# A two-layer hybrid trunk on one core: the attention layer rewritten token-major, four heads at a time, woven into its projections

## The chip, the cores and the metric
The kernel runs on one NeuronCore of a Trainium2 chip. The metric is the device time of one execution in microseconds (us); several runs are made and the median is compared. TensorE (PE) multiplies matrices into PSUM (eight banks of 512 float32 per partition), VectorE (DVE) and ScalarE (ACT) work on SBUF and PSUM, and SyncE (SP) issues the weight loads. Each engine runs its own list of instructions in order and waits on semaphores.

## The reference
256 tokens of width 1024 pass two layers, each a token mixer and a channel mixer, both after an RMS norm and with a residual add. Layer 0 is a gated linear recurrence and a dense SwiGLU; layer 1 is the attention that is changed here, and a top-2-of-8 expert SwiGLU. Then comes a last norm. The attention:

```python
qkv = h @ w_qkv + b_qkv                                   # 1024 -> 16*64 q, 4*64 k, 4*64 v
q, k = apply_partial_rope(q, cos, sin), apply_partial_rope(k, cos, sin)   # first 16 of 64 dims
scores = einsum('bnqkgd,bnjkd->bnkgqj', qb, kc) * 64 ** -0.5              # blocks of 128, own and previous
scores = where(allowed, scores, NEG_INF)                  # causal, window 128
probs = softmax(concatenate([scores, sink], -1), -1)[..., :-1]            # a learned sink per head
o = einsum('bnkgqj,bnjkd->bnqkgd', probs, vc)
return o @ w_o + b_o
```

All is float32. Four query heads share a key and value head.

## The kernel before, in words
The residual `h` lies feature-major: 8 chunks of 128 features by 256 tokens. All weights stream through a ring of 14 slots of 1 MB (a "piece" is a 1024x256 part of a weight matrix). The first part of the program uses seven of them; slots 7 to 10 serve it as scratch, and 11 to 13 hold split activations. The order of the work is written out by hand, one list per engine, with counting semaphores.

Two kinds of matmul are used. The recurrence, the attention and the router use plain float32 operands (`tile`, L1047: 8 matmuls of 128x256 for a 128x256 result; each float32 matmul shows as two instructions in the trace). The dense feed-forward part and the experts split weights and activations into a high and a low fp32r part: ACT casts a piece to `w_hi` (L469, L547), DVE subtracts to get `w_lo` (L747, L929), and TensorE makes three passes, hi*hi, lo*hi and hi*lo (`PASSES`; L1123, L1140, L1331, L1353). Three buffers (`PARTS`) hold split pieces, and a piece's split can begin once the piece three before it is used up (`parts_used`).

The stages in order: load of x and constants, rotary angles on DVE (L662 to L684) and the norm (to 29 us); the recurrence (to 136 us); 42 feed-forward pieces (to 374.5 us); norm and attention (to 537 us); norm, router and expert tables (to 568 us); eight experts of 42 pieces each; the last norm and the output. A norm is: ACT squares a chunk (L422), TensorE sums over partitions with a matrix of ones (L1038), ACT takes the root (L426), DVE the reciprocal (L708) and eight scaled chunks `hn` (L710).

The attention before: the K projection waits for `hn` and runs in `tile`; V is projected token-major with its bias by a matmul (L1174, L1178). K is copied to both halves of the partitions and rotated by constant matrices (L1182, L1185, then DVE L795 to L797). Then eight rounds, one for each pair of heads. A round projects the next pair's q (L1047), scores two heads (L1209, L1212; the two heads lie on partitions 0 to 63 and 64 to 127), adds the mask and takes row maxima on DVE (L814 to L818), exponentials on ACT (L512 to L514), normalises on DVE (L824 to L827), transposes the probabilities on TensorE (L1219), copies them on ACT (L518), rotates q (L1201), and weighs the values (L1228 to L1230). After the last round come 8 output tiles (L1047) with the residual add (L841) and the squares of the next norm between them.

The queue of the weight loads: expert pieces 0 to 6 wait for the attention's pieces to be used up, one by one, and pieces 7 to 13 for the router's first matmul, since their slots hold the attention's scratch.

## Time and profile before
| | us |
|---|---|
| median of 3 runs | 1601.21 (1601.06, 1601.21, 1609.16) |
| the profiled execution | 1610.67 |
| its span | 1608.9 |
| PE busy / DVE busy / ACT busy | 1518.0 / 1159.3 / 901.1 |
| mean granted TensorE clock | 0.969 |

The span is that of the profiled execution; 1.8 us lie around it. The median of the runs is 9.5 us under it. The page gives busy shares over the whole span; the stretch of the change is a tenth of it and has to be read on its own.

### The profile page before, as it was taken

Reading aid. Unit: us, or ns where it says so; the run is one execution under the profiler, and the core shown is the slowest. Engines: PE = TensorE matmul, PEld = TensorE weight load, DVE = VectorE, ACT = ScalarE, POOL = GpSimd, SP = SyncE. Lnnn points to the kernel's source line nnn. Section 1 sums busy time; section 2 is a strip of 40 time slices with the busy share of each in tenths; the row PEclk is TensorE's granted clock in tenths of the full one; section 3 lists DMA queues with packets and bytes.
Section 4 is the critical chain, followed back from the end, with each engine's and each line's share of the span. In section 5 each row is a group of like instructions: output and inputs, shape, how many; then the busy total and the mean of one; then the engine's idle time right before and its main releaser. Section 6 shows DMA issues by size and latency. Waiting matters only on the chain.

```text
span 1608.9 us, 25224 instructions
## 1 busy us (share of the span) xinstructions
PE 1518.0 (94%) x10533; PEld 1364.4 (85%) x10533; DVE 1159.3 (72%) x1225; ACT 901.1 (56%) x935; POOL 0.2 (0%) x4
## 2 busy tenths in 40 slices
PE   5989999998778799999999999999999999999995
PEld 4879999996556788989989898998898998898883
DVE  5564555552443488888888979979888988888883
ACT  2533444431233177676676766767767766766762
POOL 0000000000000000000000000000000000000000
PEclk9999999999879799999999999999999999999997
DMA  6436555551111589999989989999999999999910
GB/s 235 157 105 229 179 189 189 184 184 53 53 53 53 221 340 352 342 342 363 367 315 365 373 311 364 373 337 352 356 341 345 364 335 353 358 342 349 356 67 28
DMA packets 62058, 425.28 MB, mean 264 GB/s; under 512 B 7805, under 2 KB 10106, under 8 KB 10746
## 3 DMA queue, kind: packets, MB, share of 16 engines
q1 hardware_dynamic: 60240, 422.60, 70.9%
q8 instruction: 86, 1.41, 0.3%
q10 hardware_dynamic: 1706, 1.06, 0.2%
q14 instruction: 26, 0.21, 0.0%
HBM read 422.59 MB, written 1.05 MB: 263 GB/s over the span
## 4 chain that ended last, share of the span: by engine, by line
PE 90%; DVE 4%; ACT 3%; issue 2%; DMA 1%; ACTq 0%; DVEq 0%
PE ps L1331 37%; PE ps L1353 19%; PE ps L1123 10%; PE ps L1047 9%; PE ps L1140 5%; PE ps L1301 2%; PE ps L1319 2%; PE ps L1338 1%; PE ps L1038 1%; DVE w_lo L929 1%; ACT w_hi L547 1%; DVE ring L814 1%; PE ps L1178 0%; DVE hn L710 0%; PE ps L1267 0%
## 5 line engine op out<-in xcount | busy, mean ns | idle before, releaser
L929 DVE TENSOR_TENSOR w_lo<-ring,w_hi 128x2048 fp32r<-128x2048 f32 x336 | 766.4, 2290 | 126.7 <-ACT w_hi L547 121.0
L547 ACT CAST w_hi<-ring 128x2048 fp32r<-128x2048 f32 x336 | 639.5, 1909 | 264.6 <-PE ps L1331 213.5
L1331 PE MATMUL ps<-w_hi,xg_hi 128*96 128x256 f32 x1792 | 246.9, 280 | 2.5 <-ACT w_hi L547 2.5
L1331 PE MATMUL ps<-w_lo,xg_hi 128*96 128x256 f32 x1792 | 242.2, 277 | 1.6 <-DVE w_lo L929 1.6
L1331 PE MATMUL ps<-w_hi,xg_lo 128*96 128x256 f32 x1792 | 241.8, 277 | 0.0
L1331 PEld LDWEIGHTS ps<-w_hi,xg_hi 128*96 128x96 f32 x1792 | 221.6, 162 | 15.9 <-DVE xg_lo L935 2.6
L1331 PEld LDWEIGHTS ps<-w_lo,xg_hi 128*96 128x96 f32 x1792 | 215.1, 161 | 3.2 <-DVE w_lo L929 3.2
L1331 PEld LDWEIGHTS ps<-w_hi,xg_lo 128*96 128x96 f32 x1792 | 216.1, 162 | 0.0
L747 DVE TENSOR_TENSOR w_lo<-ring,w_hi 128x2048 fp32r<-128x2048 f32 x42 | 96.2, 2293 | 80.7 <-ACT w_hi L469 80.7
L469 ACT CAST w_hi<-ring 128x2048 fp32r<-128x2048 f32 x42 | 79.9, 1904 | 105.0 <-PE ps L1123 98.8
L1353 PE MATMUL ps<-w_hi,ht_hi 128*96 128x512 f32 x448 | 128.0, 407 | 0.0
L1353 PE MATMUL ps<-w_lo,ht_hi 128*96 128x512 f32 x448 | 122.4, 394 | 0.0
L1353 PE MATMUL ps<-w_hi,ht_lo 128*96 128x512 f32 x448 | 122.4, 395 | 0.0
L1047 PE MATMUL ps<-hn,ring 128*128 128x256 f32 x416 | 105.8, 419 | 13.5 <-issue 9.0
L1047 PEld LDWEIGHTS ps<-hn,ring 128*128 128x128 f32 x416 | 87.8, 213 | 30.8 <-issue 16.7
L1353 PEld LDWEIGHTS ps<-w_lo,ht_hi 128*96 128x96 f32 x448 | 71.9, 161 | 32.5 <-DVE w_lo L929 0.6
L1353 PEld LDWEIGHTS ps<-w_hi,ht_lo 128*96 128x96 f32 x448 | 72.2, 161 | 31.4
L1353 PEld LDWEIGHTS ps<-w_hi,ht_hi 128*96 128x96 f32 x448 | 63.7, 162 | 16.2
L422 ACT ACTIVATE xg_mem<-h 128x256 f32<-128x256 f32 x40 | 16.3, 415 | 76.1 <-DVE h L841 27.6
L1123 PE MATMUL ps<-u_hi,w_hi 128*128 128x256 f32 x448 | 57.5, 281 | 0.0
L1123 PE MATMUL ps<-u_lo,w_hi 128*128 128x256 f32 x448 | 57.3, 281 | 0.0
L1123 PE MATMUL ps<-u_hi,w_lo 128*128 128x256 f32 x448 | 57.3, 281 | 0.0
(235 smaller groups left out, 1373.8 us busy)
## 6 DMA issues: line engine op xcount, KB each, us to landing
ring<-in_moe_w_gate SPq DMA_DIRECT2D x112, 1024.0 KB, 5.8
ring<-in_moe_w_up SPq DMA_DIRECT2D x112, 1024.0 KB, 5.9
ring<-in_moe_w_down SPq DMA_DIRECT2D x112, 1024.0 KB, 5.8
ring<-in_ffn_w_gate SPq DMA_DIRECT2D x14, 1024.0 KB, 4.9
ring<-in_ffn_w_up SPq DMA_DIRECT2D x14, 1024.0 KB, 4.9
ring<-in_ffn_w_down SPq DMA_DIRECT2D x14, 1024.0 KB, 4.8
ring<-in_lru_w_in SPq DMA_DIRECT2D x8, 1024.0 KB, 7.9
ring<-in_attn_w_qkv SPq DMA_DIRECT2D x6, 1024.0 KB, 4.9
```

The source lines that it names most:

```text
L422: nc.scalar.activation(sq[:, c % 2], h[:, c], ACT.Square).then_inc(sq_ready, 1)
L469: nc.scalar.copy(w_hi[:, j % PARTS], ring[:, slot_of[FIRST_FFN + j]]).then_inc(hi_done, 1)
L547: nc.scalar.copy(w_hi[:, (SPLITS + n) % PARTS], ring[:, s]).then_inc(hi_done, 1)
L747: V.tensor_tensor(w_lo[:, j % PARTS], ring[:, slot_of[FIRST_FFN + j]], w_hi[:, j % PARTS].bitcast(F32), ALU.subtract).then_inc(lo_done, 1)
L929: V.tensor_tensor(w_lo[:, part], ring[:, ORDER_MOE[n % SLOTS]], w_hi[:, part].bitcast(F32), ALU.subtract).then_inc(lo_done, 1)
L1047: mm = nc.tensor.matmul(ps[:, bank, c0:c0 + T], w[:, k, col:col + P], rhs[:, k], start=(k == 0), stop=(k == KC - 1))
L1123: mm = nc.tensor.matmul(ps[:, 2 * (c % 2) + f, m * T:(m + 1) * T], w[b][:, k, f * P:(f + 1) * P], us[a][:, k], start=(k == 0 and (a, b) == ...
L1140: mm = nc.tensor.matmul(ps[:, 4 + d // 2, (d % 2) * T:(d % 2 + 1) * T], w[b][:, f, d * P:(d + 1) * P], fs[a][:, c % 2, f], start=False, st ...
L1301: mm = nc.tensor.matmul(ps[:, SCATTER_BANK[m], (d % 2) * T:(d % 2 + 1) * T], y_tok[:, d * P:(d + 1) * P], gt, start=True, stop=True)
L1319: mm = nc.tensor.matmul(ps[:, 4 + g, m * CAP:(m + 1) * CAP], hn_tok[:, b, c * P:(c + 1) * P], sel[:, b], start=(b == 0), stop=(b == TT - 1))
L1331: mm = nc.tensor.matmul(ps[0:CAP, c % 2, m * CHF:(m + 1) * CHF], xs[a][:, k], w[b][:, k], start=(k == 0 and (a, b) == (0, 0)), stop=(k == ...
L1353: mm = nc.tensor.matmul(ps[0:CAP, 2 + g, :], hs[a][:, c % 2, f], w[b][:, f, g * 512:(g + 1) * 512], start=(c == 0 and f == 0 and (a, b) == ...
```

## The change
- The norm before the attention is no longer applied ahead of the projections. ACT makes, for each chunk as it is finished, its square and `u_hi` (the chunk times the norm's weight, cast), and DVE `u_lo`; the projections run on these, and 1/rms is applied per token when their results are evicted. The sum of squares is 16 float32 matmuls with a single moving column (`mean_squares`), inside the K projection.
- All ten pieces of `w_qkv` and `w_o` go through the hi/lo split and three passes, as the feed-forward pieces do. The last feed-forward piece goes output chunk by output chunk.
- Q, K and V are projected token-major, so the bias is an operand of the eviction (loaded once, broadcast, 0.8 MB) and the rotation touches 16 of each 64 columns; the angle tables shrink from 256 columns to 16. The rotation matrices and the duplicating matrices go.
- K is written twice side by side, transposed, and stored with one half of the partitions zero, so a score matmul takes all 128 partitions. The mask is added by a bf16 matmul with the identity. Four heads of a group are scored into three PSUM banks; row maxima and exponentials read PSUM.
- Probabilities are transposed unnormalised, the values come out token-major, and one DVE instruction normalises a group. The heads are transposed back, and split into `heads_hi` and `heads_lo`.
- Four rounds instead of eight, with the Q projections, and parts of the output projections, in between, in the order listed in the diff.
- The expert loads 0 to 6 wait for the splits of attention pieces 3 to 9, and 7 to 13 for the use of the last one.

The core of the diff (`project`, `evict`, `rope`, `row_max`, `empty_probs`, `normalise`, `split_heads` and `turn_*` are as described):

```diff
-SPLITS = FFN_LOADS
+SPLITS = FFN_LOADS + ATT_LOADS
...
-                if FIRST_FFN <= last < FIRST_ATT:
+                if last >= FIRST_FFN:
                     sp.wait_ge(lo_done, last - FIRST_FFN + 1)
-                elif last >= FIRST_ATT:
-                    sp.wait_ge(used, last - FFN_LOADS + 1)
...
-                    if first and n < SLOTS:
-                        sp.wait_ge(used, LRU_LOADS + min(ATT_LOADS, ATT_LOADS - DENSE + n + 1))
+                    if first and n < DENSE:
+                        sp.wait_ge(lo_done, SPLITS - DENSE + n + 1)
+                    elif first and n < SLOTS:
+                        sp.wait_ge(parts_used, SPLITS)
...
+            split_att(0)
+            split_att(1)
+            for c in range(KC):
+                act.wait_ge(h_ready, 2 * KC + c + 1)
+                nc.scalar.activation(sq_all[:, c], h[:, c], ACT.Square).then_inc(att_sq, 1)
+                nc.scalar.activation(u_hi[:, c], h[:, c], ACT.Copy, scale=param("mix1", c)).then_inc(att_u_hi, 1)
+            split_att(2)
+            act.wait_ge(att_sum, 1)
+            nc.scalar.activation(rms2, ps[:, 7, 0:TT], ACT.Sqrt, bias=eps_col, scale=1.0 / D).then_inc(att_rms, 1)
+            split_att(3)
+            split_att(4)
+            split_att(5)
...
+            def soften(g):
+
+                st = stat[:, 64 * (g % 2):64 * (g % 2) + 64]
+                act.wait_ge(negmax, 2 * g + 1)
+                for n in range(GROUP):
+                    nc.scalar.activation(probs[:, 0, n * P:(n + 1) * P], ps[:, 2, n * P:(n + 1) * P], ACT.Exp, scale=HD ** -0.5,
+                                         bias=st[:, 8 + n:9 + n], accum_out=st[:, 16 + n:17 + n]).then_inc(exp_done, 1)
...
+            empty_q(0)
+            soften(0)
+            split_att(6)
+            empty_q(1)
+            empty_last_probs(0)
+            soften(1)
+            split_att(7)
+            empty_q(2)
+            empty_last_probs(1)
+            soften(2)
+            cast_heads(0)
+            empty_q(3)
+            empty_last_probs(2)
+            soften(3)
+            cast_heads(1)
+            cast_heads(2)
+            split_att(8)
+            empty_last_probs(3)
+            cast_heads(3)
+            split_att(9)
...
+            split_att(0)
+            split_att(1)
...
+                dve.wait_ge(att_u_hi, c + 1)
+                V.scalar_tensor_tensor(out=u_lo[:, c], in0=h[:, c], scalar=param("mix1", c), in1=u_hi[:, c].bitcast(F32),
+                                       op0=ALU.mult, op1=ALU.subtract).then_inc(att_u, 1)
+            split_att(2)
+            dve.wait_ge(att_rms, 1)
+            link(V.reciprocal(rstd2, rms2))
+            for m in range(2):
...
+            def evict(a, out, col):
+                dve.wait_ge(parts_used, FFN_LOADS + a + 1)
+                for b in range(TT):
+                    V.scalar_tensor_tensor(out=out[:, b], in0=ps[:, a % 2, b * T:(b + 1) * T].rearrange("p (h d) -> p h d", d=HD),
+                                           scalar=rstd2[:, b:b + 1], in1=bias_row[:, col:col + T].rearrange("p (h d) -> p h d", d=HD),
+                                           op0=ALU.mult, op1=ALU.add).then_inc(qkv_evac, 1)
...
+            evict(K_PIECE, k_tok, D)
+            rope(K_PIECE, k_tok)
...
+            split_att(3)
+            evict(V_PIECE, v_tok, D + NKV * HD)
+            split_att(4)
+            for g in range(2):
+                evict(Q_PIECE + g, q_tok[:, g], T * g)
+                rope(Q_PIECE + g, q_tok[:, g])
+                if g == 0:
+                    empty_k(0)
+                    empty_k(1)
+                    split_att(5)
+            row_max(0)
+            evict(Q_PIECE + 2, q_tok[:, 0], 2 * T)
+            rope(Q_PIECE + 2, q_tok[:, 0])
+            split_att(6)
+            empty_probs(0)
+            row_max(1)
+            normalise(0)
+            evict(Q_PIECE + 3, q_tok[:, 1], 3 * T)
+            rope(Q_PIECE + 3, q_tok[:, 1])
+            split_att(7)
+            empty_probs(1)
+            row_max(2)
+            normalise(1)
+            split_heads(0)
+            empty_probs(2)
+            row_max(3)
+            normalise(2)
+            split_heads(1)
+            split_att(8)
+            split_heads(2)
+            empty_probs(3)
+            normalise(3)
+            split_heads(3)
...
-                dve.wait_ge(wo_proj, c + 1)
-                V.scalar_tensor_tensor(out=h[:, c], in0=ps[:, c % 4, 0:T], scalar=param("b_o", c), in1=h[:, c],
...
+                dve.wait_ge(parts_used, FFN_LOADS + O_PIECE + c // 2 + 1)
...
+                last = c == NCH - 1
+                if last:
+                    pe.wait_ge(lo_done, j + 1)
+                    order = [(a, b, d) for d in range(KC) for a, b in PASSES]
...
+            def mean_squares():
+                pe.wait_ge(att_sq, KC)
+                for b in range(TT):
+                    for c in range(KC):
+                        mm = nc.tensor.matmul(ps[:, 7, b:b + 1], sq_all[:, c, b * P:(b + 1) * P], const("ones")[:, 0:1],
+                                              start=(c == 0), stop=(c == KC - 1))
+                mm.then_inc(att_sum, 1)
+
+            def project(a):
+                w = att_parts(a)
+                us = (u_hi, u_lo)
+                if a >= 2:
+                    pe.wait_ge(qkv_evac, 2 * (a - 2) + 2)
+                open_bank(a % 2)
+                for m, n in PASSES:
+                    if n:
+                        pe.wait_ge(lo_done, FFN_LOADS + a + 1)
+                    for k in range(KC):
+                        if a == 0 and n == 0:
+                            pe.wait_ge(att_u if m else att_u_hi, k + 1)
+                        for b in range(TT):
+                            mm = nc.tensor.matmul(ps[:, a % 2, b * T:(b + 1) * T], us[m][:, k, b * P:(b + 1) * P], w[n][:, k],
+                                                  start=False, stop=(k == KC - 1 and n == 1), skip_group_check=True)
+                    if a == 0 and m:
...
+                    if m:
+                        mask, each, heads_in = mask_bf[:, P:3 * P], 2, (2 * m - 2, 2 * m - 1)
+                    else:
...
+                    nc.tensor.matmul(ps[:, 2 + m, :], ident_bf, mask.unsqueeze(1).to_broadcast([P, each, width]),
+                                     start=True, stop=False, skip_group_check=True)
+                    for at, n in enumerate(heads_in):
+                        q_cols = slice(P, 2 * P) if m else slice(0, P)
+                        mm = nc.tensor.matmul(ps[:, 2 + m, at * width:(at + 1) * width], q_fm[:, g % 2, n // 2, q_cols],
+                                              kd[:, g, n % 2, 0:width], start=False, stop=True, skip_group_check=True)
...
+            def project_out(t, ks):
+                a = O_PIECE + t
+                w = att_parts(a)
+                hs = (heads_hi, heads_lo)
+                if 0 in ks:
+                    if t == 0:
+                        pe.wait_ge(qkv_evac, 2 * (Q_PIECE + 3) + 2)
+                    else:
+                        pe.wait_ge(exp_done, 9 * NKV)
+                    open_bank(WO_BANK[t])
+                pe.wait_ge(*emptied("h", max(ks) // 2))
+                for m, n in PASSES:
+                    if n:
+                        pe.wait_ge(lo_done, FFN_LOADS + a + 1)
+                    for f in range(2):
+                        for k in ks:
+                            mm = nc.tensor.matmul(ps[:, WO_BANK[t], f * T:(f + 1) * T], w[n][:, k, f * P:(f + 1) * P], hs[m][:, k],
+                                                  start=False, stop=(k == KC - 1 and n == 1), skip_group_check=True)
+                if KC - 1 in ks:
+                    mm.then_inc(parts_used, 1)
+
...
+            project(K_PIECE)
+            project(V_PIECE)
+            project(Q_PIECE)
+            turn_k(0)
+            turn_k(1)
+            project(Q_PIECE + 1)
+            turn_q(0)
+            score(0)
+            project(Q_PIECE + 2)
+            turn_q(1)
+            turn_probs(0)
+            score(1)
+            weigh_values(0)
+            project(Q_PIECE + 3)
+            turn_q(2)
+            turn_probs(1)
+            score(2)
+            weigh_values(1)
+            turn_heads(0)
+            turn_q(3)
+            project_out(0, (0, 1))
+            turn_probs(2)
+            score(3)
+            weigh_values(2)
+            turn_heads(1)
+            project_out(0, (2, 3))
+            turn_heads(2)
+            turn_probs(3)
+            project_out(0, (4, 5))
+            weigh_values(3)
+            project_out(1, range(6))
+            turn_heads(3)
+            project_out(2, range(6))
+            for t in range(3):
+                project_out(t, (6, 7))
+            for c in range(4):
+                sum_square(2, c, 7)
+            project_out(3, range(KC))
+            for c in range(4, KC):
+                sum_square(2, c, 7)
```

## Rows read from the trace of the kernel before
**Rows 1.** The page: granted clock in 40 slices; a costly group (busy, mean ns).
```profile
PEclk9999999999879799999999999999999999999997
...
L469 ACT CAST w_hi<-ring 128x2048 fp32r<-128x2048 f32 x42 | 79.9, 1904 | 105.0 <-PE ps L1123 98.8
```

**Rows 2.** Busy time by stretch: length, PE, PEld, DVE, ACT, POOL (instructions), clock, DMA share, GB/s.
```profile
200.00:220.00 20.00, 20.00 (x172) 20.00 (x171) 11.15 (x10) 8.53 (x8) 0.00 (x0) 1.00 0.57 204
...
374.50:544.90 170.40, 129.75 (x599) 100.94 (x598) 66.04 (x195) 45.30 (x137) 0.00 (x0) 0.87 0.17 56
...
440.90:452.60 11.70, 9.22 (x42) 6.85 (x42) 5.72 (x19) 3.92 (x14) 0.00 (x0) 0.71 0.17 50
...
544.90:551.70 6.80, 6.80 (x33) 6.80 (x33) 0.00 (x0) 0.00 (x0) 0.00 (x0) 0.50 0.75 283
...
600.00:650.00 50.00, 50.00 (x369) 45.31 (x368) 44.20 (x35) 33.60 (x27) 0.00 (x0) 1.00 0.96 355
```

**Rows 3.** Timeline, end of the dense feed-forward part: start, us, engine, line, operation.
```profile
359.78 2.29 DVE L747 TENSOR_TENSOR w_lo<-ring,w_hi 128x2048 fp32r<-128x2048 f32 x1 [3.36 <-ACT w_hi L469]
...
372.66 2.05 PE L1140 MATMUL ps<-f_hi,w_lo 128*128 128x256 f32 x16
373.33 2.74 DVE L788 TENSOR_TENSOR h<-ps,h 128x256 f32<-128x256 f32 x8 [6.80 <-PE ps L1140]
...
385.65 9.31 PE L1047 MATMUL ps<-hn,ring 128*128 128x256 f32 x32 [6.28 <-issue]
```

**Rows 4.** Timeline where the feed-forward part gets its split activations today.
```profile
118.94 0.42 DVE L754 TENSOR_TENSOR h<-ps,h 128x256 f32<-128x256 f32 x1 [2.55 <-PE ps L1047]
...
119.40 0.42 ACT L422 ACTIVATE xg_mem<-h 128x256 f32<-128x256 f32 x1 [3.47 <-DVE h L754]
...
119.79 0.48 DVE L758 SCALAR_TENSOR_TENSOR u_lo<-h,par,u_hi 128x256 fp32r<-128x256 f32 x1
```

**Rows 5.** Timeline in the attention, rounds of two heads.
```profile
419.71 0.50 PE L1209 MATMUL ps<-ring 64*128 64x128 f32 x4
...
420.04 0.61 PE L1212 MATMUL ps<-ring 64*128 64x256 f32 x4
...
421.47 0.41 DVE L817 TENSOR_REDUCE ring<-ring 128x1 f32<-128x256 f32 x1
...
422.17 0.40 ACT L512 ACTIVATE ring<-ring 128x128 f32<-128x128 f32 x1 [0.57 <-DVE ring L818]
...
422.57 0.49 ACT L513 ACTIVATE ring<-ring 128x256 f32<-128x256 f32 x1
...
424.16 5.30 PE L1047 MATMUL ps<-hn,ring 128*128 128x256 f32 x16
...
430.25 0.65 PEld L1219 LDWEIGHTS ps<-cst,ring 128*128 128x128 f32 x6 [0.33 <-issue]
...
485.69 3.72 PE L1047 MATMUL ps<-hn,ring 128*128 128x256 f32 x16
```

**Rows 6.** Timeline, the last norm and the router.
```profile
537.38 0.42 ACT L422 ACTIVATE xg_mem<-h 128x256 f32<-128x256 f32 x1 [3.47 <-DVE h L841]
...
544.88 6.97 PE L1267 MATMUL ps<-wr,hn 128*128 128x8 f32 x32 [6.33 <-DVE hn L710]
...
551.70 3.65 PE L1274 MATMUL ps<-cst,hn 128*128 128x128 f32 x16
...
552.65 0.22 DVE L858 TENSOR_TENSOR xg_mem<-small 128x64 f32<-128x64 f32 x1
...
552.87 0.57 ACT L539 COPY work<-ps 128x512 f32<-128x512 f32 x1
```

**Rows 7.** Timeline, start of the program: the rotary angles and the first evictions of x.
```profile
10.69 0.29 DVE L662 CAST ring<-ring 128x256 f32<-128x256 int32 x1
...
17.59 2.73 DVE L687 COPY h<-ps 128x256 f32<-128x256 f32 x8
```

**Rows 8.** Waits of the SyncE queue in the expert stage: total us, times, longest.
```profile
SPq L373 <- DVE w_lo L929: 489.4, 205, 5.7
```

505 lines of the change are left out of this document (251 added, 254 removed), and 3 rows, old and new, of the table TURNS.

## The prediction, made before the changed kernel was run
> **What bounds the kernel now.** I read the page's slices first [rows 1]: each is 40 us, and the granted clock dips in slices 11, 12 and 14 (402 to 563 us, the attention and the router) and at the very end; elsewhere it is near full. Busy time by stretch comes next [rows 2]. In the feed-forward part TensorE is busy 20.00 of 20 us, with 172 instructions (0.116 us each); in the experts 50.00 of 50 us. There the weight queue waits for the DVE splits that free slots, 489.4 us in 205 waits [rows 8], and not the other way round, so the loads keep ahead. The experts neither gain nor lose unless their first pieces come late. The stretch of the attention, from 374.5 to 544.9 us, is different: 170.4 us with TensorE busy 129.8, a clock of 0.87, DVE busy 66 and ACT 45. No engine is full; it is a chain of handoffs, and the low clock comes with the waits: in one round (11.7 us) TensorE is busy 9.2 us at 0.71 [rows 2]. So the change has to be priced as a chain from the end of the feed-forward part (374.5) to the router's first matmul (544.88), and all times below are on the clock of this trace.
>
> **Durations used.** A three-pass piece is 48 matmuls of 0.116 us and an opening matmul (0.2), 5.8 us; two plain tiles take 2 x 3.72 = 7.4 [rows 2, 5]. At the low clock (0.50, 1.2 GHz) a weight load of 128 columns takes 6.97/32 = 0.218 us, at the full one 0.65/6 = 0.108 [rows 5, 6], a factor of two, which I use for all matmuls. So at full clock a transpose costs 0.11, a float32 matmul with a narrow moving operand two loads, 0.22, one of 256 columns 3.72/8 = 0.465, one of 128 about 0.23. A split is 1.9 on ACT and 2.29 on DVE [rows 1, 3]. ACT empties 128x512 in 0.57 [rows 6]; for DVE I take 0.6. An exponential costs 0.40 (128 columns) and 0.49 (256), a maximum 0.41 for 256 columns, so 0.65 for 512 [rows 5]. A small DVE operation is 0.22 [rows 6]. A bf16 matmul of 512 columns has no row of its own; I take two loads, 0.21, and between 0.1 and 0.465 it moves a round by under 1 us.
>
> **Step 1, into the K projection.** Before: first residual add at 373.33, K at 385.65 [rows 3]. Now DVE must add a chunk, wait for ACT's square and cast, and subtract, and its next add is queued behind that subtraction. From the feed-forward entry [rows 4]: add to ACT start 0.46, then 0.42 twice, handoff 0.05, subtraction to next add 0.4: 1.76 us a chunk. The reordering of the last piece releases chunks from 370.5 on, but DVE first does the splits of attention pieces 0 and 1, and the second may start only when the last but one piece is used (369): ACT 1.9 and DVE 2.3 end at 373.3, so nothing is earlier. The two DMA issues that ACT makes for sinks and bias move ahead of the feed-forward pieces, where ACT waits for TensorE before its next cast; they cost nothing, nor does their 0.8 MB. Eight chunks end at 387.3. The first pass follows chunk by chunk and hides in it. The new wait on `lo_done` ahead of the last piece costs nothing: that split ends at 359.78 + 2.29 = 362.07, before the piece starts [rows 3].
>
> **Step 2, the rest of K.** TensorE has mostly waited for 13 us, so it starts low. 16 matmuls x 0.232 = 3.7; the mean squares 32 instructions, 7.0 low, 3.5 full; the last pass 3.7 low, 1.9 full. Rows for both exist: the K tiles of before rise within their 9.31 us [rows 3], while the router's 32 narrow instructions stay at 0.50 for all 6.8 us, and 16 transposes after them take 3.65 [rows 2, 6]. `mean_squares` is narrow like the router, so I take low: 14.4 us, to 401.7; bounds 9.1 and 14.4.
>
> **Step 3, to the first scores.** V and Q0 11.6, four blocks of K transposed 8 x 0.11 = 0.9, Q1 5.8, four transposes, an ACT copy and two handoffs 1.2, scores of a group 3 x 0.21 + 4 x 0.23 + 4 x 0.465 = 3.4: 22.9, to 424.6. DVE's evictions (2 x 0.48), rotation (six small operations, 1.5), K copies and splits run beside the projections, about 17 us of work in 23. The root's table load falls beside them too; where it doesn't, it costs 1.3.
>
> **Step 4, two full rounds.** A round is a projection (5.8), 16 transposes with handoffs (2.0), scores (3.4), values (12 float32 matmuls, 24 x 0.108 = 2.6). Row maxima (2.2) and exponentials (4 x 0.40 + 4 x 0.49 + 0.28 = 3.8) hide under the projection: 3.1 us of them come after the scores, against 5.8. But DVE, after the projection, evicts and rotates (2.5), splits (2.3) and empties two banks (1.2), 6.0 against TensorE's 5.4 to the values: 0.6 of wait. 14.4 each, to 453.4; heads and q transposes 0.9.
>
> **Step 5, rounds three and four.** No Q projection is left to hide the softmax, only 12 matmuls (1.4) at a time. DVE is free at 450.8: maxima 2.2, exponentials' second half 2.2, cast 0.6, subtraction 0.65, handoffs 0.2: 456.7. Matmuls 1.4, transposes 1.3, scores 3.4 (462.8), values 2.6. Tail of the maxima 0.9, then 2.2 + 0.6 + 0.65 + 0.2: 467.4, TensorE waits 1.2. 1.4 and 0.4 of matmuls and transposes: 469.2. Then a queue effect: the subtraction of heads 2 stands behind the split of piece 8 on DVE, and the third bank of transposes of round four waits for it: 0.6 + 1.9 + 2.3 + 0.65 + 0.1 gives 474.7, 5 us of wait. 1.8 and the values 2.6: 479.1. Two output pieces over six chunks 8.8 and transposes 0.4: 488.3; piece 0 is complete at 489.7.
>
> **Step 6, the tail.** The split of piece 9 needs piece 0 used up: 1.9 + 2.3 + 0.1, 494.0. Four adds stand behind it on DVE (1.6), the fourth square and sum 0.9, last piece 5.8: 502.3; two more adds, and the last square starts at 503.3. From there to the router it is 544.88 - 537.38 = 7.5 as before [rows 6]: 510.8.
>
> **Clock in the rounds.** This has TensorE at full clock from 402 on. Before, a wait of 2 to 3 us cost the next tile 5.30 - 3.72 = 1.6 us [rows 5]. I count three waits over 2 us (steps 5 and 6) and smaller ones: 6 us; bounds 0 and, at the 0.8 of the old rounds on 60 us of work, 15. Router at 516.8, 28.1 us earlier.
>
> **Start.** The angle chain on DVE, 10.69 to 17.59 [rows 7], is about 17 linked operations of 256 columns; at 0.2 each they take 3.6, and the copies of mask and identity add 0.7: 2.6 us earlier, all on the path, as the evictions of x stand behind it; bounds 0 and 4.
>
> **Expert loads.** Pieces 7 to 13 are released at 502, ahead of the router rather than with it, and take some 20 us of a DMA queue at 355 GB/s [rows 2] against 29 us to the first expert matmul: nothing.
>
> **Sum.** 28.1 + 2.6 = 30.7 us: 1610.7 gives 1580 for an execution like the profiled one. The median of the runs is 9.5 us under it and two of three agree within 0.2 us, so I take 1601.2 - 30.7 = 1570.
>
> **A rule against the change.** A pair of heads scored on two partition halves takes 419.71 to 420.65, 0.94 us [rows 5]; on the full array the same matmuls are 1.4 by the durations above, 3.6 us more over eight pairs, which is in the sum. The Trainium skill (TensorEngine Tiling (Array Packing), Theoretical Speedup) says that a contraction of 64 or less gains up to a factor of two from row tiling, which this change gives up; by it the loss is an estimated 8 x 0.94 = 7.5 us instead, and the time 1574. The case's rows show a factor of 1.5.
>
> **Rivals.** (a) *The clock comes back early*: full after step 2's first pass, no loss in the rounds, and the start gives 4: 5.3 + 6 + 1.4 = 13 less, 1557. For: TensorE's gaps are shorter than before. Against: the router's row. (b) *The elementwise chains set the rounds*: linked DVE operations and PSUM reads cost 3 us more in each of four rounds and the clock stays at the old 0.8, 12 + 9 more, 1591. For: DVE has 6.0 against 5.4 already in step 4. (c) *Slower*: TensorE stays at 1.2 GHz for the rounds, because transposes and narrow matmuls don't lift it. For: the router and the transposes after it [rows 2, 6]. Against: 288 wide matmuls of the q, k, v pieces lie between them, and the old rounds, with fewer, had 0.71 to 0.9. Price: about 84 us of TensorE work on the path doubles, less the 6 counted: 1648. It decides once 37 of the 84 us run low. The Trainium skill (TensorE: Matmul & The Clock Gate, Part 4: PE-mode transpose) says transposes don't count as busy for the clock; here 88 of them are under 10 us of the work. (d) *The gain is eaten* by several waits: within 8 us of before.
>
> **Chances.** Forecast 0.48, (a) 0.20, (b) 0.22, (c) 0.06, (d) 0.04. About 0.5% (8 us) is what a measurement can tell. Faster 0.90, same 0.04, slower 0.06. The range 1552 to 1596 takes in (a), (b) and the bounds of steps 2, the clock and the start.
>
> **What would show it.** Step 1: adds 1.7 to 1.8 us apart, K's first pass ending near 387. Step 2: the mean squares at 7 or 3.5 us. Step 4: rounds of 14 to 15 us. Step 5: a TensorE wait near 5 us for the subtraction behind the split of piece 8. The router near 517, or 514 with the start counted; the expert stage as long as before. Wrong would be rounds over 18 us, a clock under 0.7 in them, or a first expert matmul that waits for a load.

## The result and the profile after

The kernel after took 1591.8 us in the median of 8 runs (1588.5 to 1597.0), the kernel before 1602.4 (1600.9 to 1609.2): a ratio of 0.993, with 0.991 to 0.995 as its interval. It is 10.5 us faster; 31 were forecast (1570), and the time is inside the range. The profiled execution of after took 1589.4, that of before 1610.7, 21.3 apart: seven of the eight executions of before lie at 1600.9 to 1602.6 and one at 1609.2, and the profiled one, which is not among the eight, was of that upper kind.

The page of after: the span, the granted clock in 40 slices, and the groups of the feed-forward cast and of the experts' gate and up matmuls (busy us, mean ns).

```profile
span 1587.5 us, 25538 instructions
...
PEclk8999999997998899999999999999999999999997
...
L1527 PE MATMUL ps<-w_hi,xg_hi 128*96 128x256 f32 x1792 | 252.1, 282 | 2.5 <-ACT w_hi L585 2.5
L1527 PE MATMUL ps<-w_lo,xg_hi 128*96 128x256 f32 x1792 | 248.2, 279 | 0.5
...
L484 ACT CAST w_hi<-ring 128x2048 fp32r<-128x2048 f32 x52 | 99.0, 1905 | 123.5 <-PE ps L1239 98.4
```

The same groups of the experts on the page of before, which the prediction did not look at:

```profile
L1331 PE MATMUL ps<-w_hi,xg_hi 128*96 128x256 f32 x1792 | 246.9, 280 | 2.5 <-ACT w_hi L547 2.5
L1331 PE MATMUL ps<-w_lo,xg_hi 128*96 128x256 f32 x1792 | 242.2, 277 | 1.6 <-DVE w_lo L929 1.6
```

Code, shape and count are the same, and 1792 matmuls are busy 252.1 us instead of 246.9. The cast of 2048 columns did not change (1905 ns against 1904 in [rows 1]).

Busy time by stretch of after, columns as in [rows 2]: feed-forward, attention, one round, router, experts.

```profile
200.00:220.00 20.00, 20.00 (x173) 20.00 (x172) 10.51 (x10) 8.99 (x8) 0.00 (x0) 1.00 0.62 208
369.10:508.20 139.10, 114.76 (x800) 103.90 (x799) 69.23 (x140) 50.38 (x116) 0.00 (x0) 0.89 0.25 89
430.60:444.60 14.00, 14.00 (x110) 13.12 (x110) 8.47 (x22) 6.33 (x21) 0.00 (x0) 1.00 0.23 74
508.20:515.10 6.90, 6.90 (x33) 6.90 (x34) 0.00 (x0) 0.00 (x0) 0.00 (x0) 0.50 1.01 425
600.00:650.00 50.00, 50.00 (x373) 45.75 (x372) 41.47 (x33) 33.11 (x27) 0.00 (x0) 1.00 0.93 340
```

The attention went from 170.4 us to 139.1, and TensorE waits 24 us in it instead of 41. A round of four heads takes 14.0 us with TensorE busy all the time at clock 1.00, where a round of two took 11.7 at 0.71 [rows 2]. In the last window after even has more instructions than before (373, 369 in [rows 2]), though its experts are slower: 50 us hold another part of an expert, with other shapes, in each kernel. A longer stretch, 900 to 1300 us, shows the loss. Before, then after:

```profile
900.00:1300.00 400.00, 399.30 (x2912) 359.12 (x2911) 344.75 (x256) 279.80 (x237) 0.00 (x0) 1.00 0.94 352
```

```profile
900.00:1300.00 400.00, 399.77 (x2869) 360.86 (x2868) 340.28 (x255) 276.08 (x234) 0.00 (x0) 1.00 0.92 342
```

TensorE is full and its clock 1.00 in both, yet 43 instructions fewer (1.5%) fit into 400 us. The 50 us windows are useless for this, and the busy share hides it altogether. From the first expert matmul to the end of the span before took 1608.9 - 568.0 = 1040.9 us and after 1587.5 - 531.7 = 1055.8. So the account of the profiled executions is 36.3 us gained up to the first expert matmul and 14.9 lost behind it.

The timeline of after (start, duration), to be held against [rows 3, 6]: the chunks, K's second pass, the mean squares, K's third pass and V's first, the queue effect, and the router.

```profile
367.73 0.42 DVE L835 TENSOR_TENSOR h<-ps,h 128x256 f32<-128x256 f32 x1
369.03 0.48 DVE L837 SCALAR_TENSOR_TENSOR u_lo<-h,par,u_hi 128x256 fp32r<-128x256 f32 x1 [0.88 <-ACT u_hi L515]
369.43 0.42 DVE L835 TENSOR_TENSOR h<-ps,h 128x256 f32<-128x256 f32 x1
...
381.54 3.62 PE L1309 MATMUL ps<-w_hi,u_lo 128*128 128x256 f32 x16
384.95 3.89 PE L1292 MATMUL ps<-cst,hn 128*128 128x1 f32 x32
388.71 3.59 PE L1309 MATMUL ps<-w_lo,u_hi 128*128 128x256 f32 x16
...
392.57 2.18 PE L1309 MATMUL ps<-w_hi,u_hi 128*128 128x256 f32 x16
...
463.14 2.29 DVE L788 TENSOR_TENSOR w_lo<-ring,w_hi 128x2048 fp32r<-128x2048 f32 x1 [4.70 <-ACT w_hi L484]
465.35 0.68 DVE L912 TENSOR_TENSOR u_lo<-ps,u_hi 128x512 fp32r<-128x512 f32 x1
...
466.18 1.08 PE L1367 MATMUL ps<-cst,ring 128*128 128x128 f32 x4 [4.62 <-DVE u_lo L912]
...
508.17 6.96 PE L1465 MATMUL ps<-wr,hn 128*128 128x8 f32 x32 [6.30 <-DVE hn L751]
```

The adds are 1.70 us apart, since each waits behind a subtraction that waits for ACT; the wait of 4.62 us stands where DVE splits piece 8 first; the router starts 36.7 us earlier than in [rows 6].

The experts' matmuls, in blocks of 8, timeline of before and then of after; the step from one start to the next is what a block costs.

```profile
958.69 1.08 PE L1331 MATMUL ps<-w_hi,xg_hi 128*96 128x256 f32 x8
959.61 1.07 PE L1331 MATMUL ps<-w_hi,xg_lo 128*96 128x256 f32 x8
960.51 1.07 PE L1331 MATMUL ps<-w_lo,xg_hi 128*96 128x256 f32 x8
961.42 1.09 PE L1331 MATMUL ps<-w_hi,xg_hi 128*96 128x256 f32 x8
```

```profile
957.64 1.10 PE L1527 MATMUL ps<-w_hi,xg_lo 128*96 128x256 f32 x8
958.58 1.10 PE L1527 MATMUL ps<-w_lo,xg_hi 128*96 128x256 f32 x8
959.52 1.10 PE L1527 MATMUL ps<-w_hi,xg_hi 128*96 128x256 f32 x8
960.47 1.10 PE L1527 MATMUL ps<-w_hi,xg_lo 128*96 128x256 f32 x8
```

0.91 us a block before (0.1135 a matmul), 0.945 after (0.118). There are 3 x 1792 = 5376 of these matmuls; 0.0045 us each would be 24 us. The stage loses less, 15 to 16, because before has slow blocks too: of the fourteen groups of six blocks in an expert, the first behind the scatter and two or three others run at 0.93 and the rest at 0.91; after has none at 0.91. What picks these groups is open. No wait of TensorE grew to account for the loss.

### The profile page after: what moved, and what is told of

Read it like the earlier page. It is cut to its first block, busy times and chain, and to the rows that moved or that the text cites. A ratio compares the mean times of both kernels' runs of the same rounds, so it can differ in the third digit from the quotient of the medians.

```text
span 1587.5 us, 25538 instructions
## 1 busy us (share of the span) xinstructions
PE 1516.6 (96%) x10735; PEld 1382.9 (87%) x10735; DVE 1164.2 (73%) x1173; ACT 909.1 (57%) x919; POOL 0.2 (0%) x4
## 3 DMA queue, kind: packets, MB, share of 16 engines
q8 instruction: 86, 1.41, 0.3%
## 4 chain that ended last, share of the span: by engine, by line
PE 90%; DVE 5%; ACT 4%; issue 1%; DMA 1%; ACTq 0%; DVEq 0%
PE ps L1527 38%; PE ps L1549 20%; PE ps L1239 10%; PE ps L1261 5%; PE ps L1163 4%; PE ps L1309 2%; PE ps L1497 2%; PE ps L1515 2%; PE ps L1414 1%; PE ps L1534 1%; DVE w_lo L1045 1%; ACT w_hi L585 1%; PE ps L1154 1%; DVE w_lo L788 1%; PE ps L1358 0%
## 5 line engine op out<-in xcount | busy, mean ns | idle before, releaser
L1045 DVE TENSOR_TENSOR w_lo<-ring,w_hi 128x2048 fp32r<-128x2048 f32 x336 | 766.7, 2290 | 141.5 <-ACT w_hi L585 137.3
L585 ACT CAST w_hi<-ring 128x2048 fp32r<-128x2048 f32 x336 | 638.8, 1907 | 279.5 <-PE ps L1527 228.9
L1527 PE MATMUL ps<-w_hi,xg_hi 128*96 128x256 f32 x1792 | 252.1, 282 | 2.5 <-ACT w_hi L585 2.5
L1527 PE MATMUL ps<-w_lo,xg_hi 128*96 128x256 f32 x1792 | 248.2, 279 | 0.5
L1527 PE MATMUL ps<-w_hi,xg_lo 128*96 128x256 f32 x1792 | 248.0, 279 | 0.0
L1527 PEld LDWEIGHTS ps<-w_lo,xg_hi 128*96 128x96 f32 x1792 | 220.8, 161 | 2.2 <-DVE w_lo L1045 2.2
L1527 PEld LDWEIGHTS ps<-w_hi,xg_lo 128*96 128x96 f32 x1792 | 221.7, 161 | 0.0
L788 DVE TENSOR_TENSOR w_lo<-ring,w_hi 128x2048 fp32r<-128x2048 f32 x52 | 119.1, 2292 | 96.8 <-ACT w_hi L484 96.7
L484 ACT CAST w_hi<-ring 128x2048 fp32r<-128x2048 f32 x52 | 99.0, 1905 | 123.5 <-PE ps L1239 98.4
L1549 PE MATMUL ps<-w_hi,ht_hi 128*96 128x512 f32 x448 | 127.9, 407 | 0.0
L1163 PE MATMUL ps<-hn,ring 128*128 128x256 f32 x256 | 58.5, 392 | 4.5 <-DVE hn L751 3.5
L1163 PEld LDWEIGHTS ps<-hn,ring 128*128 128x128 f32 x256 | 50.3, 197 | 12.5 <-issue 5.3
L1239 PEld LDWEIGHTS ps<-u_hi,w_hi 128*128 128x128 f32 x448 | 54.7, 188 | 0.1
```

Of the source, the lines that this page charges most:

```text
L484: nc.scalar.copy(w_hi[:, j % PARTS], ring[:, slot_of[FIRST_FFN + j]]).then_inc(hi_done, 1)
L585: nc.scalar.copy(w_hi[:, (SPLITS + n) % PARTS], ring[:, s]).then_inc(hi_done, 1)
L788: V.tensor_tensor(w_lo[:, j % PARTS], ring[:, slot_of[FIRST_FFN + j]], w_hi[:, j % PARTS].bitcast(F32), ALU.subtract).then_inc(lo_done, 1)
L1045: V.tensor_tensor(w_lo[:, part], ring[:, ORDER_MOE[n % SLOTS]], w_hi[:, part].bitcast(F32), ALU.subtract).then_inc(lo_done, 1)
L1163: mm = nc.tensor.matmul(ps[:, bank, c0:c0 + T], w[:, k, col:col + P], rhs[:, k], start=(k == 0), stop=(k == KC - 1))
L1239: mm = nc.tensor.matmul(ps[:, 2 * (c % 2) + f, m * T:(m + 1) * T], w[b][:, k, f * P:(f + 1) * P], us[a][:, k], start=(k == 0 and (a, b) == ...
```

## What could make the same instructions slower

The change inserts `mask_mem` (1024 bytes a partition) ahead of `xg_hi` and shrinks the constants `cst` by 2532 bytes. Buffers lie one behind the other in the order of their declaration, each start rounded up to 32 bytes. So `xg_hi` moved from byte 162432 to 163456 and `w_hi` from 179904 to 178400, and the distance between the two operands that a gate or up matmul reads went from 17472 to 14944 bytes. `xg_lo` and `w_lo` lie 3072 and 24576 bytes behind their partners in every kernel, so all three passes have the same distance modulo 256. My theory was the alignment of w; the rivals were another effect of the addresses, and the place of the instructions in TensorE's program or the phase in which the experts start.

### Three layouts (e1, e2, e3)

e1, in the kernel after:

```diff
         table = sb("table", [1, 2 + MAX_OVER], I32)
+        sb("pad", [P, 8])
```

> The kernel after, with 32 unused bytes per partition between `table` and `w_hi`, so that `w_hi` starts at byte 178432 (a multiple of 64) instead of 178400 and `w_lo` at 203008 instead of 202976; nothing else moves. In the trace of after the attention gave 31 us and the start 5.6, but the time only 10.5: the gate and up matmuls of the experts take 0.118 us each against 0.1135 before, though their code is unchanged. Theory 1 (the address of the split weights within 64 bytes; before has 179904, a multiple of 64): blocks of 8 gate/up matmuls back at 0.907 to 0.91 us, 5376 matmuls save 15 to 25 us, time 1567 to 1576. Theory 2 (another address effect: the distance from xg to w, or xg itself): blocks stay at 0.944, time 1588 to 1597. Theory 3 (place of the instructions in TensorE's program, or the phase in which the experts start): blocks stay at 0.944, time 1588 to 1597.

e2, in the kernel after, `mask_mem` moved:

```diff
-        mask_mem = sb("mask_mem", [P, 4 * P], BF16)
...
         cst = sb("cst", [P, NCONST])
+        mask_mem = sb("mask_mem", [P, 4 * P], BF16)
+        sb("pad", [P, 376])
```

> The kernel after, with every buffer that the experts use at its address of before: `mask_mem` is put behind `cst`, and 1504 unused bytes behind it, so that xg, ht, par, small, wr, table, w_hi (179904) and w_lo (204480) start where they did. Theory 1 (alignment of w) and theory 2 (any other address effect): gate/up blocks of 8 matmuls at 0.907 to 0.91 us as in the kernel before, time 1567 to 1576. Theory 3 (instruction stream or phase): blocks stay at 0.944, time 1588 to 1597.

e3, in the kernel before, the same line as in e1:

> The kernel before, with 32 unused bytes per partition between `table` and `w_hi`, so that w_hi and w_lo start 32 bytes behind a multiple of 64, as in the kernel after; nothing else moves. Theory 1 (alignment of w within 64 bytes): gate/up blocks go from 0.91 to 0.944 us, the time from 1601 to between 1616 and 1627. Theory 2 (another address effect) and theory 3 (instruction stream or phase): within 4 us of 1601.

Measured: e1 1589.5 us (4 runs), 2 us under after, where 15 to 25 were expected of it: alignment of w to 64 bytes is not it. e2 1568.4 (1561.9 to 1575.6, 4 runs; ratio to before 0.978, 0.973 to 0.983): within 2 us of the forecast, with the changed kernel's code and the old addresses. That it comes so close is partly luck, since the four runs are two near 1562 and two near 1575, and the median lies between them. e3 1622.8 against 1603.0 for before on the same chip, a ratio of 1.010 (1.007 to 1.014): 32 bytes make the old kernel 20 us slower. The stretch of 900 to 1300 us, e2 and then e3:

```profile
900.00:1300.00 400.00, 399.19 (x2918) 359.41 (x2917) 343.73 (x258) 279.73 (x236) 0.00 (x0) 1.00 0.93 350
```

```profile
900.00:1300.00 400.00, 399.76 (x2869) 360.88 (x2868) 339.55 (x251) 275.09 (x232) 0.00 (x0) 1.00 0.93 346
```

Each kernel shows the other's count within 6. That settles that addresses do it, in both directions, and rules out the instruction stream and the phase: e2 and after hold the same instructions, and e3 and before.

A part of e2's profiled execution is not the experts'. Its feed-forward stage took 230.9 us, against 238 to 241 in all other kernels, with blocks of 16 matmuls at 1.81 instead of 1.88 to 1.90; the window of 200 to 350 us of e2 holds

```profile
200.00:350.00 150.00, 150.00 (x1326) 150.00 (x1325) 88.33 (x85) 64.97 (x66) 0.00 (x0) 1.00 0.57 195
```

and that of after x1281. Other kernels in the same layout (e9 to e12 below) have 1.88 or 1.89, so this comes and goes from one execution to the next. These are the two prices of the experts once more (0.113 and 0.118 a matmul), at one and the same layout. The distance from `u_hi` to `w_hi`, which this stage reads, is 64, 96, 128 or 192 modulo 256 in the kernels of this document, and all but this execution of e2 have 1.88 to 1.90. So in the feed-forward stage the layouts tried do not decide the price; what does is open. That the shorter feed-forward stage makes the 11 us between the two faster and the two slower runs of e2 is likely by its size, but not shown.

### Which address (e5, e6, e7)

e5 and e6 start from e2, with the line below ahead of `xg_hi`; e5 takes its 32 bytes off the pad behind `mask_mem` again, e6 doesn't. e7 is e1 with 24 in place of 8.

```diff
+        sb("pad_xg", [P, 8])
         xg_hi, xg_lo = sb("xg_hi", [P, KC, CAP], F32R), sb("xg_lo", [P, KC, CAP], F32R)
```

> The kernel after in the layout of before, but with xg_hi to ht_lo (the stationary operands of the experts) 32 bytes further on and w_hi and w_lo where they were in before. Absolute alignment of w decides: gate/up blocks stay at 0.91 us, span 1560 to 1574. The distance from the stationary operand to w, or the alignment of the stationary operand, decides: 0.944 us, span 1576 to 1592.

> The same with everything from xg_hi to w_lo 32 bytes further on, so that all distances between them are those of before. Distance decides: gate/up blocks at 0.91 us, span 1560 to 1574. Absolute alignment of w decides: 0.944 us, span 1576 to 1592.

> The kernel after with 96 unused bytes ahead of w_hi: it starts at 178496, which is 64 past a multiple of 128 as in the kernel before (179904), while 178400, 178432 and 179936, all slow, are 96, 0 and 96 past one; xg stays where after has it. If w's place within 128 bytes decides (or its distance from xg within 128 bytes, which is then that of before too): gate/up blocks at 0.91 us and a median of 1565 to 1575. If the place of xg or of w in a larger unit decides: 0.944 us and 1588 to 1597.

The pads ahead of `xg_hi` move ht, `cst` and `mask_mem` with it. Moving xg alone costs the stage 13 us, moving w alone (e3) 16, and moving both costs nothing: it is the distance between the two operands. e7 met neither expectation cleanly, with blocks of 0.91 and 0.93, a stage 4 to 5 us longer than the best, and 1579.1 us. All layouts, with the stage from the first gate or up matmul of the experts to the start of their last block of 8 (profiled execution), and the instruction count of TensorE from 900 to 1300:

```
kernel           xg_hi    w_hi     distance  mod 256  stage us  count   time us (runs)
before           162432   179904   17472      64       996.5    2912    1602.4 (8)
e2 (after)       162432   179904   17472      64       995.8    2918    1568.4 (4)
e6 (after)       162464   179936   17472      64       997.3    2909    1581.8 (1)
e13 (after)      163456   178624   15168      64       996.8    2921    1574.5 (6)
e7 (after)       163456   178496   15040     192      1001.3    2908    1579.1 (4)
e5 (after)       162464   179904   17440      32      1009.0    2880    1588.6 (1)
e1 (after)       163456   178432   14976     128      1010.8    2877    1589.5 (4)
e3 (before)      162432   179936   17504      96      1012.2    2869    1622.8 (4)
after            163456   178400   14944      96      1012.4    2869    1591.8 (8)
```

From one contraction chunk to the next the moving operand steps by 1024 bytes and the stationary one by 384, so the distance grows by 640, which is 128 modulo 256. A layout at 64 thus alternates between 64 and 192, and so does one at 192, in the other phase: the two good ones. The others never meet 64 or 192. The stage repeats well: e9 to e12, in the layout of e2, took 996.5 to 996.9, and the kernels of the two scans below, in that of after, 1012.4 each. The times of the last column do not compare as well: e5, e6 and e7 ran where before took 1609.3 in the median, and single runs differ by their attention. That of e6 took 143.7 us to the router, against 136.5 in e2, because TensorE's clock stayed at 0.50 from K's third chunk to past K's end, 24 us without a break:

```profile
375.10:398.80 23.70, 19.12 (x80) 17.29 (x81) 9.48 (x21) 8.81 (x14) 0.00 (x0) 0.50 0.13 45
```

### The two reads with nothing else at work (e4, e8)

Behind the last expert, blocks of matmuls that differ only in where their operands start (e4: 24 matmuls a block; e8: 12, and more offsets). The core of e8:

```diff
+            for cols, src, pitch in ((128, wl, 256), (96, xf, 96)):
+                for so in range(0, 128, 8):
+                    for mo in range(0, 128, 8):
+                        for r in range(12):
+                            k = r % 6
+                            (even, odd)[n_scan % 2](ps[0:cols, 0, 0:256], src[:, so + k * pitch:so + k * pitch + cols],
+                                                    wf[:, mo + k * 256:mo + (k + 1) * 256])
```

> The kernel after with 64 blocks of 24 matmuls (256 moving columns from w_hi) added behind the last expert, where no other engine works: 32 with a stationary operand of 96 columns from xg_hi, 32 with one of 128 columns from w_lo; the first column of the moving operand goes through 8 offsets of 32 bytes, that of the stationary one through 4. They add about 64 x 24 x 0.116 = 178 us. If the effect of the addresses lies in TensorE's own two reads (weights and moving operand), blocks differ by offset, 2.72 us against 2.83 (0.1135 and 0.118 a matmul), in a pattern that repeats with the offset. If it comes from DVE, ACT or DMA writing the neighbouring parts at the same time, all blocks are alike here.

> As in the scan before, behind the last expert and with no other engine at work, but 512 blocks of 12 matmuls: the first column of the stationary and of the moving operand each go through 16 offsets of 32 bytes (0 to 480), first with a stationary operand of 128 columns from w_lo (202976; both pitches 1024 bytes), then with the experts' 96 columns from xg_hi (163456, pitch 384). In the first scan the fast blocks (2.73 us for 24, against 2.80 to 2.88) lay on a diagonal: at 128 columns where the moving offset was 192 bytes more than the stationary one, at 96 columns where it was 96 more. If the distance of the two reads modulo 512 decides: 128 columns fast (1.36 us for 12 against 1.41) in 16 blocks on one wrapped diagonal and nowhere else. If it is modulo 256, on two diagonals. If the absolute address counts beside the distance, the diagonal has gaps.

In e4 most blocks took 2.80 to 2.87 us and seven 2.72 or 2.73: four with 96 columns where the moving offset is 96 bytes more than the stationary one, two with 128 columns where it is 192 more, and the first block with 96 columns and the stationary offset 32.

Three blocks of e8, with 96 columns and the stationary offset 160, moving offsets 224, 256 and 288, and the next one:

```profile
2057.31 1.57 PE L1615 MATMUL ps<-w_hi,xg_hi 128*96 128x256 f32 x12
2058.71 1.53 PE L1612 MATMUL ps<-w_hi,xg_hi 128*96 128x256 f32 x12
2060.08 1.57 PE L1615 MATMUL ps<-w_hi,xg_hi 128*96 128x256 f32 x12
2061.49 1.56 PE L1612 MATMUL ps<-w_hi,xg_hi 128*96 128x256 f32 x12
```

1.40, 1.37 and 1.41 us from start to start. The block times in units of 0.01 us for 96 columns, stationary offset down, moving offset across, in steps of 32 bytes (first half of six of the 16 rows; the second half of each repeats it within 0.01, save for the 136 at the start of row 32, which is 142 there):

```
stationary 0     142 142 140 137 141 140 140 142
stationary 32    136 142 142 140 137 141 140 140
stationary 64    140 142 141 142 141 136 141 141
stationary 96    140 140 142 141 142 141 136 141
stationary 128   141 140 140 142 141 142 141 136
stationary 160   136 141 141 139 142 142 142 140
```

The fast blocks lie on a diagonal that wraps after 256 bytes: moving offset minus stationary offset is 96, a distance of 14944 + 96 = 15040 bytes, 192 modulo 256, as in all 32 places of the scan that have it. Two more blocks are as fast without it, the first of the rows 32 and 288; the moving offset has just jumped back from 480 to 0 there. With 128 columns all 9 fast blocks (1.37 or 1.38) are at 192 modulo 256 too, but the other 23 places with that remainder are at 1.40 to 1.42, among them one of the two where e4 had its fast ones. So the modulus I expected (512) was wrong, and the gaps say that the distance is not everything. What is shown: with DVE, ACT and the weight queue idle, the same matmul with 96 stationary columns costs 0.114 or 0.118 us by the distance of its two operands. The Trainium skill (SBUF — State Buffer, "SBUF: two separate sides") places contention at the port that DVE and GpSimd share and at the DMA side alone, and gives TensorE two read ports, one for the moving operand and one for the weight load, which it calls independent. By that the distance between the two should cost nothing; in the scan, with neither of the two places at work, it costs 2 to 4%. That it is these two reads meeting in the memory is my reading; the scan doesn't show the memory. Nor does it explain why the experts do best at 64 while the idle blocks do best at 192.

### A new distance with the old remainder (e13)

e1 with 56 in place of 8, all else that of after.

> The kernel after, unchanged but for 224 unused bytes ahead of w_hi, which make the distance from xg_hi to w_hi 15168 bytes: 64 more than a multiple of 256, as 17472 was before, though 2304 bytes shorter. So far the experts' gate/up stage (first to last gate/up matmul) took 996 to 997 us at 17472 bytes (64 modulo 256), 1001 at 15040 (192), 1009 at 17440 (32), 1011 at 14976 (128) and 1012 at 14944 and 17504 (96). Theory (the distance counts modulo 256): 996 to 998 us, blocks of 8 at 0.91, and a median of 1570 to 1576 (after less 16 us; nothing is gained in the attention, where another pair of operands is read). Rival (the exact distance, or the neighbours that share the old layout): over 1001 us, and 1579 or more.

Stage 996.8 us, as forecast, and 1574.5 us in 6 runs, ratio to before 0.980 (0.976 to 0.983): 224 unused bytes are worth 17 us to the kernel after. For this stage neither the exact distance nor the neighbours matter.

## Was the attention priced rightly (e9 to e12)

Four runs in the layout of e2, on the waits that the prediction's steps 1, 2 and 5 named. For them I give the time from the end of the feed-forward stage to the router's first matmul, 139.1 us in after and 136.5 in e2. These are single executions, and nine with the attention of after took between 136.5 and 143.7, so e2 is the shortest of its kind and 2 us are nothing. The spread comes from two places: K's last matmul stands 23 us behind the feed-forward stage in six of them and 26 in three (e6, e8, e13), whose clock stayed low as shown above, and the rest differs by two or three.

e9:

```diff
             split_heads(1)
-            split_att(8)
             split_heads(2)
             empty_probs(3)
+            split_att(8)
             normalise(3)
```

> The layout of before (the run e2, router's first matmul 139 us after the feed-forward part as in after), and on DVE the split of piece 8 moved behind the subtraction of heads 2 and the two bank copies of round four. Theory (step 5 of the prediction: the wait of 4.6 us for that subtraction is a queue effect of the 2.29 us split): the wait goes, the router comes 2.3 to 4.6 us earlier after the end of the feed-forward part. Rival (the output pieces set the end: piece 8's split, now later, is waited for): the same wait turns up ahead of the output piece 8 and the router stays within 1 us.

The wait fell from 4.6 us to 0.62, in e9's timeline (1568.6 us, one run):

```profile
461.08 0.69 DVE L913 TENSOR_TENSOR u_lo<-ps,u_hi 128x512 fp32r<-128x512 f32 x1 [2.86 <-ACT u_hi L549]
...
461.91 0.63 PE L1368 MATMUL ps<-cst,ring 128*128 128x128 f32 x4 [0.62 <-DVE u_lo L913]
```

and no new wait came ahead of piece 8: the queue effect is as told. From the end of the feed-forward stage the router came only 2.0 us sooner (134.5). Ahead of the edit e9 was already 2.6 us later than e2, in part by a first pass of V at the low clock, 2.83 us against 2.15; that is not the edit's doing. What the edit is worth shows from the eight transposes just ahead of the wait: from there to the router it is 41.1 us in e9 and 45.6 to 47.6 in the ten executions with the old order, 4 to 6 us less.

e10:

```diff
-                dve.wait_ge(att_u_hi, c + 1)
-                V.scalar_tensor_tensor(out=u_lo[:, c], in0=h[:, c], scalar=param("mix1", c), in1=u_hi[:, c].bitcast(F32),
-                                       op0=ALU.mult, op1=ALU.subtract).then_inc(att_u, 1)
+                for d in ([c - 1] if c else []) + ([c] if c == KC - 1 else []):
+                    dve.wait_ge(att_u_hi, d + 1)
+                    V.scalar_tensor_tensor(out=u_lo[:, d], in0=h[:, d], scalar=param("mix1", d), in1=u_hi[:, d].bitcast(F32),
+                                           op0=ALU.mult, op1=ALU.subtract).then_inc(att_u, 1)
```

> The layout of before, and DVE adds the residual of chunk c+1 before it subtracts for u_lo of chunk c. Theory (step 1 of the prediction: the next add queues behind a subtraction that waits for ACT, 1.70 us a chunk): chunks 1.0 to 1.2 us apart, K's second pass 4 to 5 us earlier, and the router 4 to 5 us earlier after the end of the feed-forward part, or more where TensorE's clock stays up. Rival (the splits of pieces 2 and 3 or the low clock after the gap set the time): chunks closer, but the router within 1.5 us.

```profile
368.87 0.42 DVE L836 TENSOR_TENSOR h<-ps,h 128x256 f32<-128x256 f32 x1
369.85 0.42 DVE L836 TENSOR_TENSOR h<-ps,h 128x256 f32<-128x256 f32 x1
370.18 0.48 DVE L839 SCALAR_TENSOR_TENSOR u_lo<-h,par,u_hi 128x256 fp32r<-128x256 f32 x1
370.57 0.42 DVE L836 TENSOR_TENSOR h<-ps,h 128x256 f32<-128x256 f32 x1
```

The adds now alternate between 0.72 and 0.98 us, 0.85 in the mean, closer than expected, and the router comes at 130.1, 6.4 us sooner than in e2 and outside the spread (1563.6 us, one run). K's last matmul stands 16.7 us behind the feed-forward stage, 6 less than the shortest without the edit. The 1.76 us a chunk of step 1 was a queue effect too, and the change left 6 us lying there.

e11 is e9 and e10 together. e12 adds the mean squares in the gaps, in a bank of their own (3) that is opened ahead of them:

```diff
-                pe.wait_ge(att_sq, KC)
+                pe.wait_ge(att_sq, c + 1)
                 for b in range(TT):
-                    for c in range(KC):
-                        mm = nc.tensor.matmul(ps[:, 7, b:b + 1], sq_all[:, c, b * P:(b + 1) * P], const("ones")[:, 0:1],
-                                              start=(c == 0), stop=(c == KC - 1))
+                    mm = nc.tensor.matmul(ps[:, 3, b:b + 1], sq_all[:, c, b * P:(b + 1) * P], const("ones")[:, 0:1],
+                                          start=False, stop=(c == KC - 1), skip_group_check=True)
...
+                        if a == 0 and m == 0 and n == 0:
+                            mean_squares(k)
```

> The layout of before (run e2, 1568.4 us) with both edits of the two runs before: the split of piece 8 later (router 1.8 us earlier after the first residual add than in e2, 135.9 against 137.7) and the adds one chunk ahead (6.2 us earlier, 131.5). If the two add up: first add to router 129.7 us, median 1568.4 - 8.0 = 1560, range 1555 to 1566 since the executions of e2 lay 13 us apart. If they overlap (both remove a wait that the other then makes): 131.5 and 1562. If the experts' layout effect were not tied to the layout, but to where the instructions lie: gate/up blocks of 8 back at 0.944 us and 1575 or more.

> As e11, and the 32 mean-square matmuls (3.9 us in a row on the path in after, [rows 2, 6] gave 7.0 or 3.5) go into bank 3, four behind each chunk of K's first pass, where TensorE waits for the next chunk. Theory: the 3.9 us leave the path but at the low clock a chunk costs 0.8 + 0.9 us of TensorE against 0.85 between adds, so 2 to 3 us remain as gain: first add to router 127 us, median 1557. Rival (TensorE becomes the limit of the chunks): no gain, within 1 us of e11.

e11: router at 129.5, 0.6 us beyond e10. That doesn't show that the two don't add up: from the eight transposes on, e11 took 42.5 us against 46.0 in e10, so the second edit's part is there, and ahead of them it was 2.9 us slower, where both have the same code. 1559.5 us in 6 runs, ratio to before 0.972 (0.969 to 0.975). e12: router at 121.9, 7.6 us sooner, where 2 to 4 were expected:

```profile
370.22 0.50 PE L1313 MATMUL ps<-w_hi,u_hi 128*128 128x256 f32 x2
370.56 0.50 PE L1293 MATMUL ps<-cst,hn 128*128 128x1 f32 x4
...
373.77 3.76 PE L1313 MATMUL ps<-w_hi,u_lo 128*128 128x256 f32 x16
377.33 2.24 PE L1313 MATMUL ps<-w_lo,u_hi 128*128 128x256 f32 x16
```

The squares leave the path (they took 4.2 us there in e11), six of the eight chunks still run at the full clock's durations, as in e11, and K's third pass takes 2.24 us at a granted clock of 0.91 where e11 had 3.76 at 0.50. The rival, TensorE as the limit of the chunks, holds for the last two only (1.3 us each). The medians show less of it: 1556.9 in 6 runs (1554.0 to 1559.1), ratio to before 0.971 (0.969 to 0.974), not to be told apart from e11, whose runs lie between 1553 and 1565. Both beat before and after; by its median e12 is the best version, 35 us below after.

## Why the prediction was wrong

The gain forecast was 31 us and 10.5 came. In the profiled executions the forecast 30.7, plus 5.6 that came beyond it up to the first expert matmul, less 14.9 lost in the experts, makes the 21.4 between the spans; 10.8 of these are not there between the medians. Point by point:

- **The failed step is a sentence of the first part: "The experts neither gain nor lose unless their first pieces come late."** They lost 15 us in the profiled execution (1040.9 to 1055.8), with the pieces in time and no change in code, clock or waits. What it missed is that the diff moves buffers: 1024 bytes in, 2532 out. With the old distance e2 gave 1568.4 against a forecast of 1570, and e13, with another distance of the same remainder, 1574.5. The diff shows both sizes; the chance given to such a thing was none.
- Expert loads at nothing: right, nothing in the experts waited longer for a load.
- Start, 2.6 us with bounds 0 and 4: the last copy chain began at 14.60 us instead of 17.59 [rows 7], 3.0 earlier; the feed-forward stage began 5.0 earlier and ended 5.6 earlier. By this pair the term is half of what came, outside its bounds; I priced the angle chain, and not what follows it. But the stage began at 133.1 in e3, which starts as before does, and between 127.9 and 132.8 in the runs with the start of after, so single executions don't settle the size.
- Step 1, 1.76 us a chunk: 1.70, and the last subtraction ended 12.3 us behind the feed-forward stage, forecast 12.8.
- Step 2, 14.4 us with 7.0 for the mean squares: 10.7, with 3.8 for them. Of the two rows I had for narrow matmuls I took the router's; these, behind 16 wide ones, came at the other bound, 3.89/32 = 0.12 us each, and the pass behind them was slow again (3.59). The granted clock goes with it: 0.50 in the second pass, 0.93 in the mean squares, 0.53 in the third pass. The windows of after:

```profile
381.54:384.95 3.41, 3.41 (x17) 3.41 (x17) 2.23 (x1) 2.43 (x2) 0.00 (x0) 0.50 0.00 0
384.95:388.71 3.76, 3.76 (x34) 3.76 (x33) 0.06 (x1) 0.00 (x0) 0.00 (x0) 0.93 0.67 233
388.71:392.23 3.52, 3.52 (x18) 3.30 (x18) 2.02 (x4) 0.26 (x1) 0.00 (x0) 0.53 0.12 49
```

- Step 3, 22.9 us to the end of the first scores: 392.2 to 416.5, 24.3.
- Step 4, 14.4 a round: 14.05. Step 5, a wait of 5 us behind the split of piece 8: 4.62, and e9 takes it away. From the end of the first scores to the router it took 91.7 us, against 86.2 by the steps and 6 for the clock: that the 6 are the clock's was not tested.
- The router 142.3 us behind the feed-forward stage: 139.1, and 136.5 to 143.7 in the nine executions of that attention. Attention and start together brought the router 36.7 us sooner, against 30.7.
- The execution: I took a gain summed on the profiled 1610.7 off a median of 1601.2. The profiled pair differs by 21.3 us and the medians by 10.5, because before's profiled execution was 8 us over its median and after's 2.5 under its own. What the upper group of before spends these 8 us on is not known, so part of a sum made on it need not exist at the median.
- Rivals: (c) is refuted, the clock was 1.00 from the end of K up to the wait of step 5, two rounds with their transposes included. (b) gives 1591, which is the time measured, but for a wrong reason: no round was 3 us longer. (d) comes nearest in kind, a gain eaten, yet not by waits.

Still open: why 64 and not 192 suits the experts best, why some groups of blocks are slow even at 64, and why the feed-forward stage of one execution of e2 was 7 to 8 us shorter than that of its sisters.

## What to carry to other kernels

Before pricing a stage at nothing because its code is untouched, list the buffers that the diff adds, drops or resizes ahead of its operands: 224 bytes of padding were worth 17 us of 1590 here, about half of what the rewrite gave against before in a good layout (28 us in e13, 35 in e2). Where TensorE is full, compare instructions in a long window and start-to-start times of one shape, not busy shares. And before you credit an edit with 2 us in one trace, look at how far executions with the same code differ in that stretch (7 us here). When an engine serves a chain, put the instruction that releases others ahead of the one that waits: two such orders and the squares in the gaps gave 15 us between the feed-forward stage and the router (136.5 to 121.9).
